# Long runs of high and low products, and new SBUF distances between weights and input, in a float32r encoder trunk

## The reference, cut to what matters

```
for l in range(DEPTH):
    h = rmsnorm(x, norm_mix[l]);  p = h @ w_in[l]            # 2048 -> 4608
    y_b = diff_attention(q, k, v, ...)                       # 8 heads
    y_a = multiscale_pool(a_in, ...);  y_c = conformer_conv(c_in, ...)
    x = x + concatenate([y_b, y_a, y_c]) @ w_out[l]          # 2048 -> 2048
    h = rmsnorm(x, norm_ffn[l]);  gu = h @ w_ffn_in[l]       # 2048 -> 11008
    g = causal_dwconv(gu[..., :D_FF], ...)
    x = x + (silu(g) * gu[..., D_FF:]) @ w_ffn_out[l]        # 5504 -> 2048
return rmsnorm(x, final_norm)
```

## Time and profile before

| | before |
|---|---|
| median of 3 runs | 2080.88 us (2080.87 to 2081.01) |
| span of the profiled execution, first to last instruction | 2078.2 us |
| what the runs' time has beside that span | 2.7 us |
| PE busy | 2064.8 us, 99% |
| DVE busy | 1415.6 us, 68% |
| ACT busy | 1081.7 us, 52% |
| DMA | 392.66 MB, mean 189 GB/s |

### The profile page before, as it was taken

How to read it: one execution, slowest core, us unless ns; L and a number is a source line. 1 busy time by engine, 2 the same in 40 slices (tenths; PEclk the granted TensorE clock), 3 DMA queues, 4 the chain that set the end, 5 groups by cost and what they waited for, 6 DMA issues and landing times.

```text
span 2078.2 us, 32569 instructions
## 1 busy us (share of the span) xinstructions
PE 2064.8 (99%) x11564; PEld 1792.4 (86%) x11564; DVE 1415.6 (68%) x2009; ACT 1081.7 (52%) x1509; POOL 23.5 (1%) x20
## 2 busy tenths in 40 slices
PE   9999999999999999999999999999999999999998
PEld 8888888888888888888888888888888888888886
DVE  7998777676666666555489978676666676654454
ACT  6556655555555554433374566455555555544444
POOL 0001100000000000000000011000000000000000
PEclk9999999999999999999999999999999999999999
DMA  8554455655555555555666544655555655565664
GB/s 290 179 183 159 139 183 182 204 190 192 192 182 192 191 192 193 193 197 179 207 209 196 177 145 145 198 190 192 191 184 182 202 189 195 183 212 193 194 199 163
DMA packets 108944, 392.66 MB, mean 189 GB/s; under 512 B 12225, under 2 KB 12737, under 8 KB 108481
## 3 DMA queue, kind: packets, MB, share of 16 engines
q1 hardware_dynamic: 106992, 386.45, 56.6%
q10 hardware_dynamic: 1872, 5.13, 0.8%
HBM read 389.43 MB, written 2.10 MB: 188 GB/s over the span
## 4 chain that ended last, share of the span: by engine, by line
PE 99%; DMA 0%; DVE 0%; ACT 0%; ACTq 0%; issue 0%; DVEq 0%
PE bank L1179 53%; PE bank L1182 27%; PE bank L1458 4%; PE bank L1457 4%; PE bank L1456 4%; PE bank L1266 2%; PE bank L1255 1%; PE bank L1256 1%; PE bank L1257 1%; DMA x<-xT 0%; PE bank L1319 0%; PE bank L1431 0%; PE bank L1342 0%; DVE xt L1131 0%; DVE wlo L716 0%; ACT whi L364 0%
## 5 line engine op out<-in xcount | busy, mean ns | idle before, releaser
L736 DVE TENSOR_TENSOR wlo<-raw,whi 128x1024 fp32r<-128x1024 f32 x728 | 885.8, 1222 | 609.5 <-ACT whi L406 608.6
L1179 PE MATMUL bank<-xg,whi 128*128 128x512 f32 x3648 | 1135.6, 393 | 1.9 <-DVE wlo L716 1.9
L406 ACT ACTIVATE whi<-raw 128x1024 fp32r<-128x1024 f32 x728 | 764.2, 1057 | 693.3 <-PE bank L1182 558.0
L1182 PEld LDWEIGHTS bank<-xg,wlo 128*128 128x128 f32 x3648 | 685.0, 188 | 151.3
L1182 PE MATMUL bank<-xg,wlo 128*128 128x256 f32 x3648 | 720.1, 279 | 0.0
L1179 PEld LDWEIGHTS bank<-xg,whi 128*128 128x128 f32 x3648 | 552.9, 188 | 6.3 <-issue 3.3
L1179 PE MATMUL bank<-hidden,whi 128*128 128x512 f32 x688 | 213.5, 392 | 0.0
L1179 PE MATMUL bank<-mix,whi 128*128 128x512 f32 x512 | 160.7, 395 | 0.0
L1182 PEld LDWEIGHTS bank<-hidden,wlo 128*128 128x128 f32 x688 | 129.2, 188 | 28.5
L1182 PE MATMUL bank<-hidden,wlo 128*128 128x256 f32 x688 | 135.8, 279 | 0.0
L1456 PE MATMUL bank<-whi,hidden 128*128 128x512 f32 x344 | 134.6, 391 | 0.0
(11 more groups left out here) (150 smaller groups left out, 1140.8 us busy)
## 6 DMA issues: line engine op xcount, KB each, us to landing
raw<-wstream SPq DMA_DIRECT2D x729, 512.0 KB, 3.4
pw_sb<-pww ACTq DMA_DIRECT2D x2, 1024.0 KB, 7.3
outT<-xt SPq DMA_DIRECT2D x8, 256.0 KB, 2.9
x<-xT SPq DMA_DIRECT2D x2, 512.0 KB, 10.3
gains<-gain_rows ACTq DMA_DIRECT2D x1, 1024.0 KB, 6.3
raw<-wstream SPq DMA_DIRECT2D x2, 256.0 KB, 4.5
x<-xT ACTq DMA_DIRECT2D x2, 256.0 KB, 5.4
x<-xT SPq DMA_DIRECT2D x2, 256.0 KB, 7.3
```

The lines of the kernel that those rows point to most:

```text
L406: nc.scalar.activation(whi[:, s, :], raw[:, s, :], ACT.Copy).then_inc(hi_ready, 1)
L736: nc.vector.tensor_tensor(wlo[:, s, :], raw[:, s, :], whi[:, s, :], ALU.subtract).then_inc(lo_ready, 1)
L1179: nc.tensor.matmul(ps[bank][:], whi[:, s, blk * P:blk * P + P], mov, start=first, stop=False)
L1182: return nc.tensor.matmul(ps[bank][:, 0:S], wlo[:, s, blk * P:blk * P + P], mov[:, 0:S], start=False, stop=last)
```

## The change

In `group`, the high products of a whole piece (eight blocks) are issued first, then the eight low ones. Only the sorted pieces of the input projection (`rel0 < B0`) keep the pairs. Buffers move: `whi` now begins at piece 1313 and `wlo` at 1570, `xg` stays at 257, and `mix`, `hidden0` and `hidden1` begin at 2443. So `whi` has an even distance to every input and `wlo` an odd one. In `v_group` and in the last layer's `token_group`, `low_at` shifts the low half by one piece of 64 bytes, and both distances are even. 54 products whose results nobody reads (`PROBES`) are issued after the last group, into banks 0 to 3.

```diff
+PROBES = (("l" * 12, 0), ("l" * 12, 16), ("h" * 6, 16), ("hhhhllll" * 2, 16), ("hlhlhlhl", 16))
+SHIFT = 16
+OFF2 = 256
...
+        def low_at(s, l, rel):
+            moves = rel // PB in (V0, V1) or (l == LAYERS - 1 and rel >= D0)
+            return wlo[:, s, SHIFT:SHIFT + PIECE] if moves else wlo[:, s, 0:PIECE]
...
-        sb("offset1", [P, 240])
+        sb("offset1", [P, 256])
+        whi = sb("whi", [P, RING, PIECE], f32r)
+        sb("offset4", [P, 16])
+        wlo = sb("wlo", [P, RING, PIECE + 2 * SHIFT], f32r)
         raw = sb("raw", [P, RING, PIECE])
-        whi = sb("whi", [P, RING, PIECE], f32r)
-        wlo = sb("wlo", [P, RING, PIECE], f32r)
...
-        sb("offset2", [P, 240])
+        sb("offset2", [P, OFF2])
         until_last_ffn = ExitStack()
-        sb("offset3", [P, 16], f32, until_last_ffn)
...
-                    nc.vector.tensor_tensor(wlo[:, s, :], raw[:, s, :], whi[:, s, :], ALU.subtract).then_inc(lo_ready, 1)
+                    nc.vector.tensor_tensor(low_at(s, l, rel), raw[:, s, :], whi[:, s, :], ALU.subtract).then_inc(lo_ready, 1)
...
+                        turn = PB
                         if nt == NT and (batch[-1] == npieces - 1 or batch[0] == 0 and not ready):
                             order.sort(key=lambda o: (o[3], o[2]))
+                            if rel0 < B0:
+                                turn = 2
...
-                        for n in range(0, len(order), 2):
-                            pair = order[n:n + 2]
+                        for n in range(0, len(order), turn):
+                            pair = order[n:n + turn]
...
-                            wl = wlo[:, s, kk * 512:kk * 512 + 512]
+                            wl = low_at(s, l, piece0 + p)[:, kk * 512:kk * 512 + 512]
...
+            flat = hidden1[:].rearrange("p k c -> p (k c)")
+            moving, weights = flat[:, 0:2 * S], flat[:, 4 * S:]
+            pe.wait_ge(evacuated, (LAYERS - 1) * TILES + TD + 8 + CREDIT)
+            for kinds, off in PROBES:
+                for n, w in enumerate(kinds):
+                    b = 2 * (n % 2) + n // 2 % 2
+                    o = weights[:, off + b * P:off + b * P + P]
+                    wide = 2 * S if w == "h" else S
+                    nc.tensor.matmul(ps[b][:, 0:wide], o, moving[:, 0:wide], start=True, stop=True)
```

More of the change, by code:

```diff
@@ L715, in low_half @@
                 dve.wait_ge(done, count)
-                nc.vector.tensor_tensor(wlo[:, s, a:b], raw[:, s, a:b], whi[:, s, a:b], ALU.subtract).then_inc(lo_ready, 1)
+                nc.vector.tensor_tensor(low_at(s, 0, 0)[:, a:b], raw[:, s, a:b], whi[:, s, a:b], ALU.subtract).then_inc(lo_ready, 1)
             dve.wait_ge(gain_loaded, 16)
@@ L1454, in token_group @@
                             wh = whi[:, s, kk * COLS:kk * COLS + COLS]
-                            wl = wlo[:, s, kk * COLS:kk * COLS + COLS]
+                            wl = low_at(s, l, D0 + DP * g + p)[:, kk * COLS:kk * COLS + COLS]
                             nc.tensor.matmul(bank, xh, wh, start=k == 0, stop=False)
```

## The result

The changed kernel takes 2098.93 us (2098.48 to 2099.50), the kernel before 2080.95 us beside it. The ratio of after to before is 1.0088, 95% interval 1.0073 to 1.0103: 18 us slower, where 25.6 us less was forecast.

A forecast was written before the change was run, and what follows sets the result against it. The prediction took TensorE, busy 99% of the span, as the bound. Its terms, -23.7 (high and low products in runs), -2.6, +0.5 and +0.2, summed to -25.6 us: 2080.9 to 2055.3 us, range 2036 to 2088 us.

The forecast's parts named there:

- (b): High products in runs of `group`, at even distance: 226.6 ns each, as in the token-major stream of the same width.
- (c): Low products in runs of `group`, at odd distance: the fast value, 113.3 ns each; called the weakest term.
- (d): `v_group` goes from odd to even distance: 384 products, 6.7 ns less each, 2.6 us less; `token_group` unchanged.
- (e): The 208 pairs left in short turns, at mixed distances: nothing; 5 ns either way is 1.0 us.
- (f): First piece: four low products of its first half fall behind the wait for the second half, 0.5 us more.
- (g): Output projection's first piece wants all four banks earlier: 0.1 us per layer, 0.2 us more; at most 0.4 each.
- (h): Tiles complete later in last pieces, delaying ScalarE and VectorE: nothing, hidden by their lead; 23 us if uncovered.
- (i): The 54 unused products at the end: nothing, as nobody waits for them; without cover some 2 us at most.
- The steps of 6.67 ns: TensorE products cost their columns' time plus whole steps of 6.67 ns, sixteen float32 columns or 64 bytes each.
- R3: Neither order nor distance does anything in this kernel: +0.7 us, 2081.6 us; chance 0.08.
- R1: Low products in runs go on alternating, 116.7 ns on the mean: 9.8 us less, 2071 us; chance 0.15.
- R2: Low products get slower in runs, 120.0 or 126.7 ns: 2086 or 2118 us; chances 0.14 and 0.06.

The follow-up runs named there:

- the first map: The kernel before with 50 stretches of unused products behind its last group, sweeping operand distance and two orders; its time says nothing.
- e1_order: The kernel before with the order of after (eight high, then eight low products), placement kept, no unused products at the end; 2079.17 us, ratio 0.9996.
- e4_31: e1_order with high weights at distance 3 and low ones at 1 (64-byte pieces, modulo 4), token-major streams at 0; 2073.11 us, ratio 0.9966.
- e3_fine: After with low-weight slots 68 instead of 66 pieces apart and inputs moved by 6: distances 0 for high, 1 for low, modulo 4; 2090.10 us, ratio 1.0049.
- e5_30: e4_31 with one high product, then its low one, throughout, and low weights at distance 0 modulo 4; 2056.40 us, ratio 0.9886.
- e2_place: After with the pair order of before everywhere, placement and unused products kept; 2102.11 us, ratio 1.0107.
- e7_notail: After without the 54 unused products at the end; 2098.68 us, ratio 1.0090.

## Why the prediction was wrong

**(b), the step that failed first.** The forecast took 226.6 ns for a high product at an even distance from `token_group`. The row was right and its class was wrong. "Even" put together two cases that the first map parts by 6 ns, and I had two rows, one of each parity, for a quantity with four values. The positions were to be worked out from the declarations: modulo 4, they would have shown that the earlier trace rows are d = 1 and 0, that the pair order was at 3, and that after brings 2 into play, of which no row told anything. A high product came to 230.7 ns on `xg` and 232.1 on `mix` and `hidden0`, and not to 226.6. Even at d = 0 it would not have been reached. In the eight-and-eight order `e1_order` and `e4_31`, with high weights at d = 3, have 1.83 us for eight, and `e3_fine`, with d = 0 everywhere, 1.84.

```profile
421.14 1.84 PE bank L1187 x8
422.98 0.94 PE bank L1190 x8
```

The row of one long stream doesn't hold for a short run. In `e3_fine` the first four high products behind a low run take 231.9 ns on the mean, from start to start, and the last three 226.4.

**(c), mis-sized by as much.** Low products were taken at 113.3 ns and came to 117.6 on `xg`, 117.3 on the mean of all. The reason that I gave for the fast value was that the alternation comes from switching widths, which the runs do less often. `e1_order` refutes it: with the distances kept and four times fewer switches, the low runs alternate still, 0.91 and 0.94 us. At the new distances on `xg` nearly all are 0.94, and at (3, 1) in `e4_31` nearly all are 0.91. So the distances decide whether the runs take the fast value, the slow one, or both in turn. A steady run of 32 takes 117.8 to 119.7 ns a product.

(b) and (c) together: a pair at 348 ns, forecast 339.9, so +3 instead of -5.1 ns. Over 4640 pairs (b) is off by 4.4 ns, some 20 us, and (c) by 4.0 ns, some 19 us. With 4.9 us for `token_group` and 0.8 for `v_group` this covers, within 1 us, the 44.7 us between the forecast span (2078.2 - 25.6 = 2052.6 us) and the measured one (2097.3).

The forecast pair exists, at another order and other distances: `e5_30` has 340.0 ns, about 227 + 113. That its time, 2056.4 us, is near the forecast of 2055.3 doesn't bear the forecast out.

**`token_group`, charged at nothing, cost 4.9 us.** The forecast said "was even and stays so". It went from d = 0 to 2 in its high halves.

**(d)** was right in kind, 1.8 us for 2.6. Its streamed low halves alternate between d = 0 and 2, again for the 66 pieces between slots.

**(e)** lies inside its bound. At the new placement the pair order costs 2.9 ns more a pair on `xg` (347.9 in `e2_place`, 345.0 before), 0.6 us for the 208, where the bound was 1.0.

**(f)** misread its rows. The products from 7.95 us are the whole first piece, and the wait that ends at 11.29 is for the second. High-first leaves nothing behind it, and the term should have been nothing. The second piece of `e1_order`, with the same order, starts at 11.32 us. In the profiled execution of after it starts at 11.97, because ScalarE waited longer for a part of `x`:

```profile
8.80 0.51 ACT L368 ACTIVATE xg<-x,par 128x256 fp32r<-128x256 f32 x1 [1.24 <-DMA x<-xT]
```

The +0.7 us that the expectations for `e3_fine` and `e4_31` carry on from there was no cost of the change: their second pieces start at 11.14 and 11.15 us.

**(g) and (h)** can't be seen in a total: `e1_order`, which has both, can't be told from before, and VectorE's idle time in after stayed at 614 us. So (h), up to 23 us if uncovered, was covered. **(i)** was right, by `e7_notail`.

**The steps of 6.67 ns** held for the steady streams at d = 0 and 1 and for the pair at 340.0 ns (51 steps). They don't hold for 229.6 and 232.5 ns at d = 3 and 2, or for 117.8. As a rule for what values a product can take they were wrong. The row that was said to fit N/2.4 + 2.5 ns (the Trainium skill, "TensorE: Matmul & The Clock Gate", "Back-to-back issue gap") has 216 ns at 256 columns, for which the formula gives 109.2; 216 is its value for 512. That row was thus no bound for a high product.

**The rivals.** R3 and the rule of the Trainium skill ("TensorE: Matmul & The Clock Gate", "Step-by-step: what each phase is for"), by which loading the next weights takes nothing from the running product, are refuted for this kernel. Order kept and only distances changed: +22 us. R1's cause, low runs that go on alternating, is what `e1_order` shows, not after: 117.3 ns is near its 116.7, but the runs on `xg` don't alternate. R2, the side on which the time came out, named low products at 120 ns as its cause. They did get slower, by 1.5 ns on `xg` against before, but stayed below its break-even of 118.8. The rest of the loss came from the high products and `token_group`, which R2 kept at the forecast. No rival had distances that count modulo four.

What stays open is why the distance modulo 256 bytes matters, and why the order chooses the best one. That the load of the next weights and the streaming input get in each other's way would be one explanation; no run here tests it.

## What to carry to other kernels

In this kernel, where TensorE is the bound and each float32r product has its own load of weights, the byte distance between stationary and streamed operand and the order of wide and narrow products had to be tuned as one. Other types and shapes were not measured. Changing one while holding the other gave 1% losses on either side of a 1.1% gain. Don't extrapolate from two rows to a rule on parity: append a few hundred unused products that sweep distance and order to the kernel, read the map off one trace, and then confirm the best cells in the kernel itself, since cells of the map were up to 4 ns a pair off. Hold the distance for every slot of a ring and every input, by padding slots to a multiple of 256 bytes; `e3_fine`, which does this, is 9 us under after.

## What the runs showed that was not expected

- A 512-column float32r product with a 128-column load beside it takes 226.7, 232.9, 232.5 or 229.6 ns in a steady run, for distances of 0, 64, 128 or 192 bytes modulo 256 between its operands.
- Two placements with the same parity differ by 9 us in the whole kernel (2098.9 and 2090.1 us).
- Two high and two low products, or one and one, differ by -45 us at one placement and +23 us at another (2101.3 to 2056.4; 2080.2 to 2102.9 us).
